# Hybrid S5 and mixture-of-experts step: the last batch's scatters ahead of slot 2's gather, slot 2's high products ahead of slot 1's low-weight products

## The chip, the core and the metric

The kernel runs on one core of a Trainium2 chip. The metric is the device time of one execution in microseconds. The engines named here are TensorE (PE in the rows), VectorE (DVE), ScalarE (ACT), GpSimd (POOL) and SyncE (SP), which here only issues transfers. Each engine works through its own instructions in the order in which the program writes them, and waits on semaphores for the others.

## The reference, cut to what matters

One decoder layer on 2112 tokens (2048 of a prompt, 64 of samples), width 1024, in float32: RMSNorm, a state-space mixer, a residual add, and then a mixture of experts in two levels with a final RMSNorm. The part that the change touches is the mixture:

```python
g_idx = jnp.argmax(pg, axis=-1)                # one of 4 groups
top_w, top_i = lax.top_k(pe, TOP_K)            # 2 of the 4 experts in it
eid = g_idx[:, None] * EXPERTS_PER_GROUP + top_i
h = silu(x @ w_gate[e]) * (x @ w_up[e])        # 1024 -> 256, for each of 16 experts
h = h * combine                                # weight of the token for that expert
out = h @ w_down[e]                            # 256 -> 1024
y = rmsnorm(x + out)
```

## The kernel before

The mixer comes first and ends in `x_mid` in HBM, the rows of all tokens, 17 tiles of at most 128 rows. In between, VectorE works out for each tile which two experts each token has and at which place in that expert's list the token stands.

**Records.** For each token and choice a record of five words (token, where the sum stands, where the output goes, weight, root) is written by an indirect transfer of GpSimd into a table `records` in HBM (`file_rows`, line 548). There are two such scatters for a tile, 34 in all, in four batches: tiles 0 to 5, 6 to 10, 11 to 14, and 15 and 16. A batch waits for the semaphore `idx_done`, which VectorE raises at line 2035 when the places (`at_rec`, line 2034) are known. SyncE reads columns of the table back into SBUF (`tab`, a part of `low`) in four loads, lines 453, 456, 458 and 459: the first two hold the records of slots 0, 1 and 2, since the places of the experts' first blocks fill up before all tiles are in; the last two hold the rest and wait until every scatter has landed.

**Slots.** The expert stage runs over slots of 128 rows, each of one expert. For slot `s`:

- `gather(s)` (line 575) on GpSimd takes the record column by `fetch` (line 564) and gathers 128 rows of `x_mid` into `xg`, ring of 8.
- `e_turn(s)` (line 1329) on TensorE transposes the rows in 8 matmuls against the identity (line 1338). For slot 1 it is `second_turn` (line 1349).
- `e_x(s)` (line 939) on ScalarE rounds the transposed rows to `xgH`, and `e_x_lo` on VectorE writes the remainder `xgL`. The weights are split likewise, into `WH` by `cut_hi` on ScalarE and `WL` by `cut_lo` on VectorE.
- The product up is a sum of three: `WH`*`xgH`, `WL`*`xgH` and `WH`*`xgL`, 8 matmuls each. In `e_up` these are `up_high` (the first two, lines 1404 and 1405) and `up_low` (line 1411). For slot 1 they are apart: `up_second_hi` (line 1359), and `up_second_lo` (lines 1365 and 1368).
- `e_silu`, `e_h` give `hh`; `e_hturn` (line 1418) transposes it in two matmuls (line 1423); `e_ht_hi` on ScalarE and `e_ht` on VectorE (line 1894) make `hTH` and `hTL`, and `e_down` (lines 1430 to 1432, 12 matmuls) gives the product down. VectorE adds it to the row (`e_sum`, line 2146), GpSimd scatters sums and outputs.

**The entry.** The first slots are written out by hand, since routing is still going on beside them. Their order is fixed by the program text alone; no scheduler moves anything. On TensorE, after the product down of slot 0, the text is: wait for the control words (`ctl_done`), transpose slot 2, the second half of slot 1's `WH`*`xgH`, then slot 1's `WH`*`xgL` and `WL`*`xgH`, slot 2's `up_high`, the transposes of slot 1's `hh`, slot 2's `up_low`, and slot 1's product down. On ScalarE, line 1002 (`cut_hi(0, 2)`, the third part of expert 1's weights) stands behind waits for all scatters, and `e_x(2, 0)` behind it. From slot 3 on `e_step` repeats.

Of the kernel before, what the change touches and what calls it, by code (L numbers as in the profile page):

```python
# [32 lines left out]
EPS = 1e-6  # L33
# [22 lines left out]
NEAR = 4 * TT  # L56
# [15 lines left out]
def hybrid_kernel(nc, x_rows, x_first, x_cols, s0, par, bc_in, d_in, gmix, gffn, gfin, w_in, w_out, w_route,  # L72
# [9 lines left out]
    with outer:  # L82
# [110 lines left out]
        for n in (0, 1):  # L193
# [68 lines left out]
        names = """par_in gm_in bc_in win0 win1 win2 win3 win4 win5 win6 win7 rt_in gl_in dch act_small c_g1 c_pool   # L262
# [5 lines left out]
            dchd exp_d consts tab_set tab_clear d_ready pos_done pos_read idx_done tab_early tab_in tab_first tab_ready tot_done words_set words_done ctl_done exp_in rec_set  # L268
# [38 lines left out]
        def _(sp):  # L307
# [150 lines left out]
            sp.dma_start(tab[:, 2:NEAR, :], table[:, 2:NEAR, :]).then_inc(S["tab_first"], 16)  # L458
# [9 lines left out]
        def _(pool):  # L468
# [5 lines left out]
            pool.memset(epsc[:, :], EPS).then_inc(S["c_pool"], 1)  # L474
            pool.memset(ones[:, :], 1.0).then_inc(S["c_pool"], 1)
# [88 lines left out]
            def fetch(t):  # L564

                if t == 3:
                    pool.wait_ge(S["tab_first"], 48)
                    pool.wait_ge(S["ctl_done"], 1)
                if t == AHEAD:
                    pool.wait_ge(S["tab_ready"], 16)  # L570
                col = pool.value_load(ctrl[0:1, C_COL + t:C_COL + t + 1], min_val=0, max_val=REC * (COLS - 1)) if t > 2 else (0, TT * REC, REC)[t]
                pool.tensor_copy(recs[:, t, :], tab[:, :, :].rearrange("p c w -> p (c w)")[:, ds(col, REC)]).then_inc(S["rec_set"], 1)
                pool.wait_ge(S["rec_set"], t + 1)
# [19 lines left out]
            for n, (lo, hi) in enumerate(BATCHES):  # L593
                if n == 2:

                    pool.wait_ge(S["tab_first"], 16)
                    pool.wait_ge(S["ys_lo"], 2 * TF)
                    for b in range(2):
                        pool.wait_ge(S[f"x2_st{b}"], 32 * ((FIRST_TOK + 1 - b) // 2) + 32 * (1 - b))
                    gather(0)  # L600

                    pool.wait_ge(S["a_done"], 4 * TF - 1)
                    gather(1)
                if n == 3:

                    pool.wait_ge(S["tab_first"], 32)
                    for b in range(2):
                        pool.wait_ge(S[f"x2_st{b}"], 32 * ((SECOND_TOK + 1 - b) // 2) + 32 * (1 - b))
                    gather(2)
                for t in range(lo, hi):  # L610
                    file_rows(t, n)

            pool.wait_ge(S["rl_evac"], TT)
# [94 lines left out]
        def _(act):  # L708
# [73 lines left out]
            act.wait_ge(S["c_pool"], 2)  # L782
# [217 lines left out]
            act.wait_ge(S["ctl_done"], 1)  # L1000
            act.wait_ge(S["wts2"], 32)
# [79 lines left out]
            e_x(2, 0)  # L1081
# [14 lines left out]
        def _(pe):  # L1096
# [77 lines left out]
            pe.wait_ge(S["c_pool"], 2)  # L1174
# [186 lines left out]
            def up_second_lo():  # L1361

                pe.wait_ge(S["xgt_lo"], 4)
                for k in range(KD):
                    pe.matmul(pbig[:, 6, :], xgL[1][:, k, :], WH[:, k * 2 * DE:(k + 1) * 2 * DE], start=False, stop=False)
                for k in range(KD):
                    pe.wait_ge(S["lo_split"], PIECES + k + 1)
                    mm = pe.matmul(pbig[:, 6, :], xgH[1][:, k, :], WL[:, EW + k * 2 * DE:EW + (k + 1) * 2 * DE], start=False, stop=(k == KD - 1))
# [212 lines left out]
        def _(dve):  # L1581
# [355 lines left out]
            dve.wait_ge(S["consts"], 10)  # L1937
# [283 lines left out]
            e_h(1, 1)  # L2221
            e_sum(0, 0)
            cut_lo(0, EW, 1, UP_CUTS)
            e_ht(1, 1)
# [77 lines left out]
```

## Time and profile before

| | us |
|---|---|
| median of 3 runs | 820.11 (818.72 to 821.96) |
| profiled execution | 819.82 |
| its span in the trace | 818.1 |
| TensorE busy in the span | 783.8 (96%) |
| VectorE busy | 597.6 (73%) |
| ScalarE busy | 409.8 (50%) |
| GpSimd busy | 341.4 (42%) |

The span is the time from the first to the last instruction in the trace; the profiled execution's time is 1.7 us longer than its span. The stage of the mixer ends and the stage of the slots begins between 405 and 450 us from the span's start; the last matmul is at 805 us. A row of the timeline gives the start, the time from start to end, the engine and line, and in square brackets the idle time of the engine before it with what ended it. Matmuls overlap, so the time between two starts is what one of them costs.

### The profile page before, as it was taken

To read this page: it belongs to the slowest core of one execution; us is meant where nothing else is said; L and a number is where in the kernel's file an instruction comes from. 1 tells how busy PE (TensorE), PEld (TensorE's weight loads), DVE (VectorE), ACT (ScalarE), POOL (GpSimd) and SP (SyncE) were. 2 spreads that over 40 slices of the span, in tenths; PEclk is the share of its full clock that TensorE was granted. 3 is DMA by queue.
4 is the path that set the end of the run, shared out by engine and by line. 5 is a ranking of instruction groups with operands and counts; after the bars stand their busy time and mean duration, and the time that the engine had idled before them with its cause. 6 is when DMAs were issued, how large, how long until landed. Compare 5 with 4: busy or idle time off the path is not lost.

```text
span 818.1 us, 15245 instructions
## 1 busy us (share of the span) xinstructions
PE 783.8 (96%) x4265; PEld 618.2 (76%) x4265; DVE 597.6 (73%) x1143; ACT 409.8 (50%) x770; POOL 341.4 (42%) x416
## 2 busy tenths in 40 slices
PE   6999989999999999999989999999999999999993
PEld 4888866655787787878767778888888888888882
DVE  7998789996543364556877598678786788776863
ACT  7556752124343543434353576546565566565632
POOL 3920011012000000322445567686766767676653
PEclk9999999999999999999999999999999999999997
DMA  8565315889742423424357588767866678877832
GB/s 306 159 228 185 129 28 186 215 160 209 287 155 81 152 107 126 133 101 155 105 208 250 184 302 259 249 208 248 273 224 227 231 260 285 291 238 233 280 121 106
DMA packets 57671, 161.27 MB, mean 197 GB/s; under 512 B 21856, under 2 KB 26464, under 8 KB 50912
## 3 DMA queue, kind: packets, MB, share of 16 engines
q1 hardware_dynamic: 34304, 112.99, 43.5%
q0 software_dynamic: 22976, 47.05, 16.5%
q8 instruction: 44, 0.72, 0.4%
q14 instruction: 59, 0.48, 0.2%
q10 hardware_dynamic: 288, 0.03, 0.0%
HBM read 129.07 MB, written 62.40 MB: 234 GB/s over the span
## 4 chain that ended last, share of the span: by engine, by line
PE 43%; POOL 2%; issue 2%; DVE 2%; DMA 1%; ACT 1%; DVEq 0%; POOLq 0%; ACTq 0%
PE pbig L1404 9%; PE pbig L1411 9%; PE pbig L1405 9%; PE pbig L1430 4%; PE pbig L1432 4%; PE pbig L1431 4%; PE pbig L1338 4%; POOL records L556 1%; PE pbig L1423 1%; DMA records<-rec,at_rec 1%; ACT xgH L944 0%; ACT pbig L1013 0%; DMA low<-records 0%; DVE fo L2137 0%; DVE xg L2146 0%
## 5 line engine op out<-in xcount | busy, mean ns | idle before, releaser
L1404 PE MATMUL pbig<-WH,xgH 128*128 (+1 forms) x304 | 123.0, 405 | 1.5 <-ACT xgH L944 0.9
L556 POOL DMA_INDIRECT records<-rec,at_rec x34 | 39.2, 1153 | 191.4 <-DVEq L2035 159.1
L1405 PE MATMUL pbig<-WL,xgH 128*128 (+1 forms) x304 | 118.9, 391 | 0.0
L1285 PE MATMUL pbig<-w2H,ysH 128*128 128x512 f32 x256 | 105.3, 411 | 0.0
L2042 DVE SCALAR_TENSOR_TENSOR WL<-WR,gf_p,WH 128x512 f32 (+1 forms) x128 | 87.4, 745 | 18.2 <-ACT WH L934 18.1
L1286 PE MATMUL pbig<-w2L,ysH 128*128 128x512 f32 x256 | 100.6, 393 | 0.0
L1287 PE MATMUL pbig<-w2H,ysL 128*128 128x512 f32 x256 | 100.5, 393 | 0.0
L630 POOL DMA_INDIRECT x_sums<-xg,recs x36 | 76.2, 2118 | 24.3 <-DVE xg L2146 13.1
L934 ACT ACTIVATE WH<-WR,gf_p 128x512 f32 (+1 forms) x128 | 81.8, 716 | 1.3
L952 ACT ACTIVATE sl<-pbig,recs 128x256 f32<-128x256 f32 x40 | 19.0, 475 | 117.8 <-PE pbig L1411 117.8
L1411 PE MATMUL pbig<-WH,xgL 128*128 (+1 forms) x304 | 77.1, 395 | 0.0
L1404 PEld LDWEIGHTS pbig<-WH,xgH 128*128 128x128 f32 x304 | 57.1, 188 | 15.3 <-issue 2.5
L1411 PEld LDWEIGHTS pbig<-WH,xgL 128*128 128x128 f32 x304 | 57.0, 188 | 13.6
L1430 PE MATMUL pbig<-WH,hTH 128*128 (+1 forms) x160 | 66.4, 415 | 0.5 <-DVE hTL L1894 0.5
L1405 PEld LDWEIGHTS pbig<-WL,xgH 128*128 128x128 f32 x304 | 57.0, 188 | 11.3
L1914 DVE TENSOR_TENSOR x<-pbig,sg 128x1024 f32<-128x1024 f32 x16 | 19.6, 1223 | 62.8 <-PE pbig L1287 61.4
L1432 PE MATMUL pbig<-WH,hTL 128*128 (+1 forms) x160 | 63.3, 396 | 0.0
L2137 DVE SCALAR_TENSOR_TENSOR fo<-xg,eroot,low 128x1024 f32<-128x1024 f32 x39 | 49.9, 1278 | 18.1 <-POOL eroot L653 18.1
L1431 PE MATMUL pbig<-WL,hTH 128*128 (+1 forms) x160 | 62.5, 390 | 0.0
L2146 DVE SCALAR_TENSOR_TENSOR xg<-pbig,recs,xg 128x1024 f32<-128x1024 f32 x39 | 49.9, 1278 | 15.1 <-PE pbig L1432 13.6
L1285 PEld LDWEIGHTS pbig<-w2H,ysH 128*128 128x128 f32 x256 | 48.2, 188 | 13.8 <-issue 4.6
L1880 DVE TENSOR_TENSOR xgL<-pbig,xgH 128x512 fp32r<-128x512 f32 x80 | 51.3, 681 | 8.0 <-ACT xgH L944 3.1
(356 smaller groups left out, 1710.6 us busy)
## 6 DMA issues: line engine op xcount, KB each, us to landing
WR<-in_w_gu SPq DMA_DIRECT2D x32, 1024.0 KB, 6.6
WR<-in_w_dn SPq DMA_DIRECT2D x16, 1024.0 KB, 5.9
xT<-in_x_cols SPq DMA_DIRECT2D x16, 512.0 KB, 3.8
low<-in_x_rows SPq DMA_DIRECT2D x16, 512.0 KB, 4.5
U<-in_x_rows SPq DMA_DIRECT2D x16, 512.0 KB, 5.3
x_mid<-x SPq DMA_DIRECT2D x16, 512.0 KB, 2.7
x_sums<-x SPq DMA_DIRECT2D x16, 512.0 KB, 4.5
w<-in_w_out SPq DMA_DIRECT2D x1, 4096.0 KB, 13.6
```

Of the source, the lines that this page charges most:

```text
L630: pool.indirect_dma_start(sumD, bass.IndirectOffsetOnAxis(ap=recs_u[:, t, SUM_AT:SUM_AT + 1], axis=0), xg[t % RING][:, :], None, bounds_ch ...
L934: act.activation(WH[:, ds(to + k * 2 * DE, 2 * DE)], WR[:, k * 2 * DE:(k + 1) * 2 * DE], ACT.Copy, scale=gf_p[:, k:k + 1]).then_inc(S["hi_ ...
L1285: pe.matmul(pbig[:, n, :], ysH[b][:, k, :], w2H[n][:, k, :], start=(k == 0), stop=False)
L1286: pe.matmul(pbig[:, n, :], ysH[b][:, k, :], w2L[n][:, k, :], start=False, stop=False)
L1287: mm = pe.matmul(pbig[:, n, :], ysL[b][:, k, :], w2H[n][:, k, :], start=False, stop=(k == CB - 1))
L1404: pe.matmul(out, xgH[b][:, k, :], WH[:, ds(off + k * 2 * DE, 2 * DE)], start=(k == 0), stop=False)
L1405: pe.matmul(out, xgH[b][:, k, :], WL[:, ds(low_ + k * 2 * DE, 2 * DE)], start=False, stop=False)
L1411: mm = pe.matmul(out, xgL[b][:, k, :], WH[:, ds(off + k * 2 * DE, 2 * DE)], start=False, stop=(k == KD - 1))
L1430: pe.matmul(out, hTH[b][:, k, :], WH[:, w], start=(k == 0), stop=False)
L1431: pe.matmul(out, hTH[b][:, k, :], WL[:, ds(low_ + at, 512)], start=False, stop=False)
L1432: mm = pe.matmul(out, hTL[b][:, k, :], WH[:, w], start=False, stop=(k == 1))
L2042: stt(WL[:, ds(low_ + w, 2 * DE)], WR[:, w:w + 2 * DE], gf_p[:, k:k + 1], WH[:, ds(to + w, 2 * DE)].bitcast(F32), ALU.mult, ALU.subtract). ...
```

## The change

Four places of the program text differ.

1. GpSimd: `gather(2)` (with its `fetch`) stood ahead of the fourth batch's four scatters; it now stands behind them. For that the third load of the table raises a semaphore of its own, `tab_near`, and two semaphores of the start (`c_pool`, `consts`) are made one.
2. ScalarE: `e_x(2, 0)` goes ahead of the last part of the weights' rounding, `cut_hi(0, 2)` and of its wait `wts2`. The waits for all scatters and for `ctl_done` still stand ahead of both.
3. TensorE: `up_second_lo` is cut in two: `up_second_x` (`WH`*`xgL`) and `up_second_w` (`WL`*`xgH`). Slot 2's `up_high` now comes between them, and the transposes of slot 1's `hh` come behind slot 2's `up_low` and straight ahead of slot 1's product down. The transposes of slot 2 (`e_turn(2, 2)`) stay where they were.
4. VectorE: `e_h(1, 1)` comes behind `e_sum(0, 0)` and the third part of `cut_lo`.

```diff
             sp.wait_ge(S["tab_in"], 16 * 2 * (TT - SECOND_TOK))
-            sp.dma_start(tab[:, 2:NEAR, :], table[:, 2:NEAR, :]).then_inc(S["tab_first"], 16)
+            sp.dma_start(tab[:, 2:NEAR, :], table[:, 2:NEAR, :]).then_inc(S["tab_near"], 16)
...
                 if t == 3:
-                    pool.wait_ge(S["tab_first"], 48)
+                    pool.wait_ge(S["tab_near"], 16)
...
-                if n == 3:
-
-                    pool.wait_ge(S["tab_first"], 32)
-                    for b in range(2):
-                        pool.wait_ge(S[f"x2_st{b}"], 32 * ((SECOND_TOK + 1 - b) // 2) + 32 * (1 - b))
-                    gather(2)
                 for t in range(lo, hi):
                     file_rows(t, n)
 
+            pool.wait_ge(S["tab_first"], 32)
+            for b in range(2):
+                pool.wait_ge(S[f"x2_st{b}"], 32 * ((SECOND_TOK + 1 - b) // 2) + 32 * (1 - b))
+            gather(2)
             pool.wait_ge(S["rl_evac"], TT)
...
             act.wait_ge(S["ctl_done"], 1)
+            e_x(2, 0)
             act.wait_ge(S["wts2"], 32)
             cut_hi(0, 2)
...
-            e_x(2, 0)
             e_silu(1, 1)
...
             up_second_hi(KD // 2, KD)
-            up_second_lo()
+            up_second_x()
             up_high(2, 0, EW, 0, 0)
+            up_second_w()
+            up_low(2, 0, EW)
             e_hturn(1, 1)
-            up_low(2, 0, EW)
             e_down(1, 1, 0, 1, EW)
...
             e_x_lo(2, 0)
-            e_h(1, 1)
             e_sum(0, 0)
             cut_lo(0, EW, 1, UP_CUTS)
+            e_h(1, 1)
             e_ht(1, 1)
```

GpSimd before, from the gather of slot 1 (`xg<-x_mid,low`) to the gather of slot 3; `records` is the table in HBM, `recs` the column taken from it:

```order
L588 DMA xg<-x_mid,low 128x1024
L572 COPY recs<-low 128x5
L556 DMA records<-rec,at_rec 34816x5 x8
L572 COPY recs<-low 128x5
L588 DMA xg<-x_mid,recs 128x1024
L556 DMA records<-rec,at_rec 34816x5 x4
L571 TENSOR_LOAD ctrl
```

GpSimd now, the same place:

```order
L588 DMA xg<-x_mid,low 128x1024
L572 COPY recs<-low 128x5
L556 DMA records<-rec,at_rec 34816x5 x12
L572 COPY recs<-low 128x5
L588 DMA xg<-x_mid,recs 128x1024
L571 TENSOR_LOAD ctrl
```

The four scatters of the fourth batch have joined the eight of the third, and the gather of slot 2 (`xg<-x_mid,recs`) has gone behind all twelve.

TensorE before, from the last matmul of slot 0's product down to the first pair of slot 2's `up_high`:

```order
L1432 MATMUL pbig<-WH,hTL0 128x512
L1338 MATMUL pbig<-ident,xg2 128x128 x8
L1359 MATMUL pbig<-WH,xgH1 128x512 x4
L1365 MATMUL pbig<-WH,xgL1 128x512 x8
L1368 MATMUL pbig<-WL,xgH1 128x512 x8
L1404 MATMUL pbig<-WH,xgH0 128x512
```

TensorE now, at the same place (line numbers of the changed program; the number behind a name is the buffer, and `xgH1` is slot 1's, `xgH0` slot 2's):

```order
L1433 MATMUL pbig<-WH,hTL0 128x512
L1336 MATMUL pbig<-ident,xg2 128x128 x8
L1357 MATMUL pbig<-WH,xgH1 128x512 x4
L1363 MATMUL pbig<-WH,xgL1 128x512 x8
L1405 MATMUL pbig<-WH,xgH0 128x512
```

The eight transposes of slot 2 are still the first thing behind slot 0's product down; what has left the place behind `WH`*`xgL` are the eight `WL`*`xgH` of slot 1.

TensorE before, from the last pair of slot 2's `up_high` to the start of slot 1's product down (`hTH`):

```order
L1404 MATMUL pbig<-WH,xgH 128x512
L1405 MATMUL pbig<-WL,xgH 128x512
L1423 MATMUL pbig<-ident,hh 128x128 x2
L1411 MATMUL pbig<-WH,xgL 128x512 x8
L1430 MATMUL pbig<-WH,hTH 128x512
```

TensorE now:

```order
L1405 MATMUL pbig<-WH,xgH 128x512
L1406 MATMUL pbig<-WL,xgH 128x512
L1369 MATMUL pbig<-WL,xgH 128x512 x8
L1412 MATMUL pbig<-WH,xgL 128x512 x8
L1424 MATMUL pbig<-ident,hh 128x128 x2
L1431 MATMUL pbig<-WH,hTH 128x512
```

Slot 1's eight `WL`*`xgH` stand behind `up_high` now, and between the transposes of `hh` and the product down that uses them no matmul is left.

## Rows read from the trace of the kernel before

**Rows 1.** The page: busy time by engine.
```profile
PE 783.8 (96%) x4265; PEld 618.2 (76%) x4265; DVE 597.6 (73%) x1143; ACT 409.8 (50%) x770; POOL 341.4 (42%) x416
```

**Rows 2.** Stretches: span, PE, PEld, DVE, ACT, POOL busy (instructions), granted clock, DMA, GB/s.
```profile
445.00:453.00 8.00, 7.34 (x36) 5.43 (x34) 2.75 (x5) 2.98 (x6) 4.71 (x7) 1.00 1.00 371
453.00:500.00 47.00, 45.34 (x215) 36.24 (x216) 38.94 (x52) 30.97 (x52) 30.78 (x32) 1.00 0.70 244
500.00:804.00 304.00, 303.99 (x1477) 249.14 (x1476) 232.92 (x297) 172.04 (x295) 208.51 (x217) 1.00 0.71 237
```

**Rows 3.** Timeline of TensorE, from slot 2's transposes to slot 1's product down.
```profile
433.08 1.03 PE L1338 MATMUL pbig<-ident,xg 128*128 128x128 f32 x8
...
434.89 2.02 PE L1365 MATMUL pbig<-WH,xgL 128*128 128x512 f32 x8
436.75 2.00 PE L1368 MATMUL pbig<-WL,xgH 128*128 128x512 f32 x8
439.20 0.51 PE L1404 MATMUL pbig<-WH,xgH 128*128 128x512 f32 x1 [0.45 <-ACT xgH L944]
...
443.02 0.38 PE L1423 MATMUL pbig<-ident,hh 128*128 128x128 f32 x2
443.15 2.11 PE L1411 MATMUL pbig<-WH,xgL 128*128 128x512 f32 x8
445.10 0.39 PE L1430 MATMUL pbig<-WH,hTH 128*128 128x512 f32 x1
```

**Rows 4.** Timeline of GpSimd: third batch's scatters, gather 2, fourth batch's.
```profile
410.46 1.02 POOL L556 DMA_INDIRECT records<-rec,at_rec  x1 [5.12 <-DVEq L2035]
...
420.39 0.96 POOL L556 DMA_INDIRECT records<-rec,at_rec  x1 [0.30 <-issue]
421.65 0.96 POOL L556 DMA_INDIRECT records<-rec,at_rec  x1 [0.31 <-issue]
427.94 0.19 POOL L572 COPY recs<-low 128x5 f32<-128x5 f32 x1 [5.33 <-DMA low<-records]
428.41 1.00 POOL L588 DMA_INDIRECT xg<-x_mid,recs  x1 [0.27 <-POOL recs L572]
429.71 0.98 POOL L556 DMA_INDIRECT records<-rec,at_rec  x1 [0.30 <-issue]
...
434.03 1.02 POOL L556 DMA_INDIRECT records<-rec,at_rec  x1 [0.30 <-issue]
```

**Rows 5.** Timeline of VectorE: the places of the third and the fourth batch.
```profile
409.44 0.17 DVE L2034 SCALAR_TENSOR_TENSOR at_rec<-high,place 128x8 uint32<-128x8 f32 x1
...
424.69 0.17 DVE L2034 SCALAR_TENSOR_TENSOR at_rec<-high,place 128x4 uint32<-128x4 f32 x1
```

**Rows 6.** Line 588: time from issue to landing of gather 2.
```profile
DMA to landing us min/median/max: 4.5/4.5/4.5
```

**Rows 7.** The same of gather 0, issued at 402.5, gather 1 behind it.
```profile
DMA to landing us min/median/max: 5.6/5.6/5.6
```

**Rows 8.** The same of gather 3, issued at 440.4.
```profile
DMA to landing us min/median/max: 7.8/7.8/7.8
```

**Rows 9.** Timeline of SyncE: the third load of the table, the weights of expert 2.
```profile
436.20 0.33 SPq L458 DMA_DIRECT2D low<-records  x1
...
437.10 0.85 SPq L443 DMA_DIRECT2D WR<-in_w_gu  x2
```

**Rows 10.** Timeline of ScalarE, behind the transposes of slot 1's hh.
```profile
443.43 0.38 ACT L958 ACTIVATE hTH<-pbig 128x256 fp32r<-128x256 f32 x1 [3.92 <-PE pbig L1423]
```

**Rows 11.** Timeline of VectorE, the same place.
```profile
443.85 0.42 DVE L1894 TENSOR_TENSOR hTL<-pbig,hTH 128x256 fp32r<-128x256 f32 x1
```

**Rows 12.** Timeline of TensorE: its longest wait between matmuls, and its last matmul.
```profile
12.97 0.50 PE L1115 MATMUL pbig<-w1H,xH 128*128 128x512 f32 x1 [1.73 <-ACT xH L722]
...
804.66 0.39 PE L1432 MATMUL pbig<-WH,hTL 128*128 x1
```

**Rows 13.** One stretch behind the last matmul, columns as in the second group.
```profile
808.00:809.00 1.00, 0.00 (x0) 0.00 (x0) 0.36 (x1) 0.00 (x0) 0.81 (x2) 0.53 0.00 0
```

More of the change, by code:

```diff
@@ L259, in hybrid_kernel @@
         wst.close()
-        names = """par_in gm_in bc_in win0 win1 win2 win3 win4 win5 win6 win7 rt_in gl_in dch act_small c_g1 c_pool
+        names = """par_in gm_in bc_in win0 win1 win2 win3 win4 win5 win6 win7 rt_in gl_in dch act_small c_g1
             x_in0 x_in1 xrow_in0 xrow_in1 w1_hi w1_lo xh_done xl_done sq_done std_done rin_done um_done us_done us8_in tr_done ue_act ue_dve
@@ L267, in hybrid_kernel @@
             wout_in w2_hi w2_lo ys_hi ys_lo a_done sig_done x2_done xr_in0 xr_in1 x2_st0 x2_st1 wr_scaled xt_done xt_evac lt_done lt_evac fold_set rl_done rl_evac ssq_done half_ss dchc
-            dchd exp_d consts tab_set tab_clear d_ready pos_done pos_read idx_done tab_early tab_in tab_first tab_ready tot_done words_set words_done ctl_done exp_in rec_set
+            dchd exp_d consts tab_set tab_clear d_ready pos_done pos_read idx_done tab_early tab_in tab_first tab_near tab_ready tot_done words_set words_done ctl_done exp_in rec_set
             gat0 gat1 gat2 gat3 xgt_done xgt_evac xgt_lo gu_done h_done sl_done ht_done ht_evac hi_split lo_split dn_done dn_evac wts0 wts1 wts2
@@ L473, in _ @@
             ch(pool.memset(power[:, :], -0.5))
-            pool.memset(epsc[:, :], EPS).then_inc(S["c_pool"], 1)
-            pool.memset(ones[:, :], 1.0).then_inc(S["c_pool"], 1)
+            pool.memset(epsc[:, :], EPS).then_inc(S["consts"], 1)
+            pool.memset(ones[:, :], 1.0).then_inc(S["consts"], 1)
             ch(pool.memset(upper[:, :], 1.0))
@@ L781, in _ @@
             act.activation(AN[:, 4, :, :], AN[:, 2, :, :], ACT.Sin).then_inc(S["act_small"], 1)
-            act.wait_ge(S["c_pool"], 2)
+            act.wait_ge(S["consts"], 2)
             for t in range(1, TA):
@@ L1172, in e_spread @@
                 mm.then_inc(S["et_done"], 1)
-            pe.wait_ge(S["c_pool"], 2)
+            pe.wait_ge(S["consts"], 2)
             a_first()
@@ L1359, in up_second_hi, with up_second_x @@
                     pe.matmul(pbig[:, 6, :], xgH[1][:, k, :], WH[:, k * 2 * DE:(k + 1) * 2 * DE], start=(k == 0), stop=False)
-            def up_second_lo():
+            def up_second_x():
                 pe.wait_ge(S["xgt_lo"], 4)
@@ L1365, in up_second_lo, with up_second_w @@
                     pe.matmul(pbig[:, 6, :], xgL[1][:, k, :], WH[:, k * 2 * DE:(k + 1) * 2 * DE], start=False, stop=False)
+            def up_second_w():
                 for k in range(KD):
@@ L1936, in _ @@
             dch = Chain(dve, S["dchd"])
-            dve.wait_ge(S["consts"], 10)
+            dve.wait_ge(S["consts"], 2 + 10)
             dch(dve.memset(logit[LAST:P, 0, :], 0.0))
```

## The prediction

> **What bounds the kernel now.** I read the page's busy times first: TensorE is busy for 96% of the span, no other engine above 73% [rows 1]. Such a share is a mean, so the stretches come next. From 500 to 804 us TensorE is busy for 303.99 of 304 us at the full clock; from 445 to 500 it lacks only 0.66 + 1.66 = 2.3 us [rows 2]. Whatever delays TensorE before 445 us therefore arrives at the end nearly whole, and whatever lets it go earlier is gained nearly whole. The change touches 425 to 450 us, so its worth is read from the order of things on TensorE there. That timeline is dense: slot 2's transposes start at 433.08 straight behind slot 0's product down, and the one wait up to slot 1's product down at 445.10 is 0.45 us before slot 2's first product, for `xgH` from ScalarE [rows 3]. By starts: the eight matmuls of `WL`*`xgH` take 1.86 us (as the eight of `WH`*`xgL` do, 434.89 to 436.75), and 436.75 + 1.86 = 438.61, so the wait costs 0.59 us. The chain of waits goes back from this wait over the fourth batch's scatters and GpSimd's gather of slot 2 to routing, and so makes GpSimd look like the bound of this place. It is so only for 0.59 us. What else hangs on GpSimd is the gather itself: issued at 428.41 [rows 4], landed 4.5 us later [rows 6], at 432.9. TensorE asks for it at 433.08. So gather 2 has a spare of 0.2 us and no more.
>
> **GpSimd: scatters ahead of the gather.** The four scatters wait for `at_rec`. In the third batch VectorE ended it at 409.44 + 0.17 = 409.61 and the first scatter began at 410.46, 0.85 us later. The fourth batch's ends at 424.69 + 0.17 = 424.86 [rows 5], so the first scatter would begin at 425.7, in an idle time of GpSimd of 5.33 us [rows 4]. From start to start undisturbed scatters take 1.26 us (420.39 to 421.65), so the fourth begins at 425.7 + 3.8 = 429.5 and ends at 430.5. If they stretch as they did before, 434.03 - 429.71 = 4.3 us instead of 3.8, it is 431.0. Then comes the copy of the record, 0.47 us from its start to the gather's (427.94 to 428.41): the gather is issued at 431.0 (to 431.5), 2.6 us later than before. The load of the column it needs had come at 427.9 and is no limit.
>
> How long does it take to land? Alone it took 4.5 us [rows 6]. Now it has company. The last scatter would land by 429.5 + 2.2 = 431.7 (before: issued 434.03, and SyncE's load of the table that waits for it began at 436.20 [rows 4, 9]), and the two loads of the table move at the same time as the gather's rows, where before they went out after it had landed. Bounds: 4.5 us alone; 7.8 us for gather 3, which had the table and two megabytes of weights beside it [rows 8, 9]. The nearest case is gather 0, with another gather of its size behind it: 5.6 us [rows 7]. I take 5.5. It lands at 436.5 and the transposes start at 436.6, 3.5 us later than 433.08. With 4.5 us it would be 2.4 to 2.9 us late, with 7.8 it would be 5.8.
>
> TensorE executes in order, and `e_turn(2, 2)` is still its first work behind slot 0's product down. Behind it stand slot 1's second half of `WH`*`xgH`, its `WH`*`xgL` and `WL`*`xgH`, all of which could run, and none can pass it. So the 3.5 us are a wait and nothing fills it.
>
> The Trainium skill, page "DMA: Bandwidth & Descriptors", section "Queues, rings and completion order", says that each transfer engine takes turns between the queues that have work for it. By that rule the gather shares with the two table loads and is slower than alone; by the row of gather 2 alone it would not be. The rows of gathers 0 and 3 side with the page.
>
> **TensorE and ScalarE: slot 2's high products first.** With the wait for all scatters gone 4 us earlier, ScalarE begins `e_x(2, 0)` as soon as the transposes are there, and about 2.9 us of matmuls (half of `WH`*`xgH` and `WH`*`xgL`) cover it. So the 0.59 us go away. From the start of the transposes to that of slot 1's product down it took 445.10 - 433.08 = 12.02 us. Without the wait and without the two transposes of `hh` (443.02 to 443.15, 0.13) that leaves 11.3 us of matmuls. Then come the transposes of `hh`, now with nothing behind them to cover what follows: `hTH` began 0.41 us after their start and took 0.38 [rows 10], `hTL` began at 443.85 and ended at 444.27 [rows 11], plus 0.06 us for TensorE to go on, in all 1.3 us from their start to the product down. Sum 11.3 + 1.3 = 12.6, or 12.5 without the slower first matmul behind the old wait: 0.5 us more than before. The change takes away one wait of 0.59 and makes one of about 1.2 (1.3 less the transposes' own 0.13). Bounds: 0 if all of it is covered after all, 1.0 if VectorE is late with `hTL`.
>
> **The rest at nothing.** ScalarE's `cut_hi(0, 2)` ends some 2 us later than before, about 440; `WL`'s third part follows on VectorE by 443, and slot 1's product down needs it at 449. VectorE's `e_h(1, 1)` moves behind the sum and that part: slot 1's product up ends only at about 445.7 now, so nothing waits for the order. `hh` is ready by 446.8, while `up_low` of slot 2 runs to 447.6. If that cover were gone (VectorE 1 us later) it would cost nothing still. The table's last loads and so gathers 3 and 4 go 4 us earlier; gather 3, issued at 440.4, landed at 448.2, just when it was wanted, and has spare now. The merged semaphore costs nothing: the same two increments are awaited.
>
> **The sum.** 3.5 + 0.5 = 4.0 us. The profiled execution is 819.82 us, its span 818.1, and the 1.7 us between them stay. So 823.8; the median of the runs is 820.11, 0.3 above it, and I predict 824.1. A measurement of this kernel can tell about 0.5%, 4.1 us, from no change: the forecast stands at that line.
>
> **Rivals.**
> *The clock falls in the wait.* The longest wait of TensorE between its matmuls was 1.73 us [rows 12], and the clock stayed full. Behind its last matmul, begun at 804.66, the granted clock has a mean of 0.53 in 808 to 809 [rows 13]: it fell to 1.2 GHz 3 us after the work had ended. A wait of 3.5 us reaches that. The work behind it then runs at half speed until the clock is back. If that lasts as long as the fall took, 3 us, it costs 1.5; if it lasts over everything up to `up_high` (436.75 - 433.08 = 3.7 us of work), 3.7. I take 2: 826.1. For it speaks the tail; against it that the wait lies between two dense stretches, which the tail does not. By the Trainium skill, page "TensorE: Matmul & The Clock Gate", section "Why this matters for your kernels", gaps in TensorE's work between bursts of matmuls can bring it back to half rate, and a wait of this size would be such a gap; the tail agrees, and the wait of 1.73 us was too short to show it.
>
> *The gather lands as late as gather 3.* 7.8 us: 5.8 + 0.5 = 6.3, 826.4. For it: scatters and two loads in flight. Against it: the weights of expert 2 wait for VectorE and would join only at its end.
>
> *Absorbed.* The gather is hardly late (the scatters' descriptors are made faster beside an idle VectorE, it lands in 4.5 us), and some of the 2.3 us of waits from 445 to 500 go: 2.5 + 0.5 - 1.5 = 1.5, 821.6. Against it: those waits are for `hh` and `xgH`, which follow TensorE itself.
>
> *Faster: the gather in time.* If the scatters' data is out of the way and the gather's rows come before TensorE has done with slot 0, the wait at the transposes is nought, the 0.59 goes, the gap before the product down is covered, and with gathers 3 and 4 and the weights 2 to 4 us earlier all 2.3 us of later waits go too: 2.9 less, 817.2. It decides at a landing by 433.1, 2.1 us after an issue at 431.0; the shortest gather here took over 4.
>
> **How the numbers follow.** Forecast 55% (its own range 822.7 to 825.2), clock 25%, late gather 8%, absorbed 7%, faster 5%. Slower by over 0.5% (above 824.2): 0.4 of the forecast's 55, nine tenths of the clock's 25, the late gather: 0.22 + 0.22 + 0.08 = 0.52. Faster: 0.05. Within 0.5%: 0.43. Range for 8 in 10: 822.0, between absorbed and the forecast's low end, to 827.0, above the clock and the late gather.
>
> **What would show it.** TensorE's row of slot 2's transposes has a wait of 2.4 to 4.5 us, for the gather; gather 2 is issued near 431.0, behind four scatters from 425.7; `up_high` of slot 2 has no wait for `xgH`; the first matmul of slot 1's product down has one of about 1 us, for `hTL`; from 500 us on everything is the same, shifted. A granted clock below 1.00 near 437 shows the first rival. No wait at the transposes, or a gather issued before 430, would prove the forecast wrong; so would waits of 2 us gone between 445 and 500.

## The result and the profile after

The changed kernel takes 823.22 us (median of 20 runs, 820.96 to 829.35), the kernel before 820.65 (20 runs beside them). The ratio is 1.0036, with a 95% interval from 1.0023 to 1.0049: slower by 0.36%, or 3.0 us. That is the forecast's direction, 0.9 us below the predicted 824.1, inside its range, and on this side of the 0.5% line.

The profiled execution took 824.25 us with a span of 822.5, 4.4 us more than the span before, and the busy times are nearly those of [rows 1]:

```profile
PE 785.8 (96%) x4265; PEld 619.2 (75%) x4265; DVE 597.9 (73%) x1143; ACT 409.8 (50%) x770; POOL 338.6 (41%) x416
```

The two spans can't be subtracted as they stand. Slot 0's product down, the last work on TensorE ahead of the change's place, begins at 430.18 us in the trace before and here at 432.36: 2.18 us of the 4.4 had arisen before the place where the orders differ. Over the thirteen traces of this study that start lies anywhere from 429.21 to 435.15 us, so what the merged semaphore of the start does to it, if anything, can't be told. So I measure every kernel of this study from that start. The *entry stretch* runs from the start of slot 0's product down to the start of slot 1's.

TensorE after, start, time, line, and the idle time with its cause, where [rows 3] stood before:

```profile
432.36 0.50 PE L1431 MATMUL pbig<-WH,hTH 128*128 128x512 f32 x1
...
437.37 1.07 PE L1336 MATMUL pbig<-ident,xg 128*128 128x128 f32 x8 [1.97 <-issue]
438.19 1.18 PE L1357 MATMUL pbig<-WH,xgH 128*128 128x512 f32 x4
439.21 2.02 PE L1363 MATMUL pbig<-WH,xgL 128*128 128x512 f32 x8
441.07 0.40 PE L1405 MATMUL pbig<-WH,xgH 128*128 128x512 f32 x1
...
444.76 2.01 PE L1369 MATMUL pbig<-WL,xgH 128*128 128x512 f32 x8
446.61 2.04 PE L1412 MATMUL pbig<-WH,xgL 128*128 128x512 f32 x8
448.49 0.38 PE L1424 MATMUL pbig<-ident,hh 128*128 128x128 f32 x2
449.80 0.50 PE L1431 MATMUL pbig<-WH,hTH 128*128 128x512 f32 x1 [0.93 <-DVE hTL L1896]
```

Three things are to be seen. TensorE waits 1.97 us at slot 2's transposes. The matmul at 441.07, slot 2's first product, waits for nothing. The product down at 449.80 waits 0.93 us for `hTL`. The entry stretch is 449.80 - 432.36 = 17.44 us; before it was 445.10 - 430.18 = 14.92. The place costs 2.52 us.

The wait at the transposes is written "issue", the name for a wait whose releaser the profile doesn't show. GpSimd tells what it is ([rows 4] before):

```profile
427.29 0.96 POOL L556 DMA_INDIRECT records<-rec,at_rec  x1 [2.58 <-DVEq L2037]
...
431.08 0.95 POOL L556 DMA_INDIRECT records<-rec,at_rec  x1 [0.31 <-issue]
432.03 0.20 POOL L572 COPY recs<-low 128x5 f32<-128x5 f32 x1
432.51 1.00 POOL L588 DMA_INDIRECT xg<-x_mid,recs  x1 [0.27 <-POOL recs L572]
```

The four scatters stand between 427.29 and 432.03, 1.26 us from start to start, and gather 2 behind them. Its time from issue to landing ([rows 6]):

```profile
DMA to landing us min/median/max: 4.8/4.8/4.8
```

432.51 + 4.8 = 437.3, and the transposes start at 437.37. The chain that ended last has the wait as a link of its own, which before it had not at this place:

```profile
435.40 1.97 issue
437.37 1.07 PE pbig L1336 x8
```

The granted clock of the wait and of the work behind it, and of the dense part ([rows 2]):

```profile
433.00:439.00 6.00, 4.03 (x23) 3.15 (x22) 5.87 (x10) 0.88 (x2) 0.64 (x2) 1.00 0.79 233
504.00:808.00 304.00, 303.88 (x1474) 248.84 (x1473) 232.78 (x297) 171.88 (x294) 207.46 (x216) 1.00 0.71 237
```

The clock stayed at 2.4 GHz through the wait, and behind 504 us all is as it was, shifted.

### The profile page after: what moved, and what is told of

It reads as the page before. It is cut to its first block, busy times and chain, and to the rows that moved or that the text cites. A ratio compares the mean times of both kernels' runs of the same rounds, so it can differ in the third digit from the quotient of the medians.

```text
span 822.5 us, 15244 instructions
## 1 busy us (share of the span) xinstructions
PE 785.8 (96%) x4265; PEld 619.2 (75%) x4265; DVE 597.9 (73%) x1143; ACT 409.8 (50%) x770; POOL 338.6 (41%) x416
## 4 chain that ended last, share of the span: by engine, by line
PE 43%; DVE 4%; issue 2%; ACT 1%; POOL 0%; DVEq 0%; ACTq 0%; POOLq 0%
PE pbig L1405 9%; PE pbig L1412 8%; PE pbig L1406 8%; PE pbig L1431 4%; PE pbig L1433 4%; PE pbig L1432 4%; PE pbig L1336 4%; PE pbig L1424 1%; DVE fo L2139 0%; ACT pbig L1012 0%; ACT WH L932 0%; PE pbig L1363 0%; PE pbig L1369 0%; ACT WH L935 0%; DVE xg L2148 0%
## 5 line engine op out<-in xcount | busy, mean ns | idle before, releaser
L628 POOL DMA_INDIRECT x_sums<-xg,recs x36 | 74.1, 2058 | 23.2 <-DVE xg L2148 13.8
L621 POOL DMA_INDIRECT xg<-x_sums,recs x36 | 49.9, 1385 | 17.6 <-issue 12.9
```

The lines of the kernel that those rows point to most:

```text
L628: pool.indirect_dma_start(sumD, bass.IndirectOffsetOnAxis(ap=recs_u[:, t, SUM_AT:SUM_AT + 1], axis=0), xg[t % RING][:, :], None, bounds_ch ...
```

## The experiments

All numbers of the kernels side by side, from one profiled execution each; the last column is the ratio to the kernel before with its interval where the kernel was timed. Starts are those of products down: "entry" from slot 0's to slot 1's, "2 to 3" from slot 2's to slot 3's, "to last" from slot 0's to the last matmul of all.

| kernel | wait at slot 2's transposes | entry | 2 to 3 | to last | ratio |
|---|---|---|---|---|---|
| before | none | 14.92 | 17.83 | 374.48 | |
| e9_before_again | none | 14.92 | 17.44 | 373.73 | |
| after | 1.97 | 17.44 | 17.02 | 376.63 | 1.0036 [1.0023, 1.0049] |
| e1_gpsimd_alone | 1.68 | 16.05 | 17.01 | 374.82 | 1.0020 [0.9998, 1.0042] |
| e2_other_engines_alone | none | 16.06 | 17.00 | 375.94 | 1.0015 [0.9995, 1.0034] |
| e3_tensore_undone | 2.02 | 16.41 | 17.10 | 374.89 | |
| e4_turn_behind | none | 14.19 | 17.03 | 373.19 | 0.9991 [0.9975, 1.0007] |
| e5_two_ahead | none | 14.36 | 16.99 | 373.42 | 0.9987 [0.9970, 1.0004] |
| e7_table_later | 1.68 | 17.18 | 17.03 | 375.74 | |
| e6_act_first | none | 14.29 | 17.54 | 373.22 | |
| e11_act_first_timed | none | 14.23 | 17.70 | 373.45 | 0.9994 [0.9982, 1.0007] |
| e8_two_ahead_act_first | none | 14.19 | 17.01 | 372.53 | 0.9983 [0.9969, 0.9998] |
| e10_gather_later | 4.70 | 22.48 | 17.04 | 382.53 | |

The entry stretch of the kernel before came out at 14.92 twice, so its tenths mean something. "To last" differs by 0.75 us between two traces of one and the same kernel, so there only differences above that do.

### One half of the change at a time

My theory, A in the expectations: gather 2 is late by the scatters, and the order on TensorE adds a gap. The rival, B: the order on TensorE is what costs. The first experiment keeps GpSimd's change alone (TensorE's part of the edit is shown; `e_x(2, 0)` on ScalarE and `e_h(1, 1)` on VectorE are back in their old places too):

```diff
 after, with TensorE, ScalarE and VectorE in the order of before:
-            up_second_x()
-            up_high(2, 0, EW, 0, 0)
-            up_second_w()
-            up_low(2, 0, EW)
-            e_hturn(1, 1)
+            up_second_x()
+            up_second_w()
+            up_high(2, 0, EW, 0, 0)
+            e_hturn(1, 1)
+            up_low(2, 0, EW)
```

> The kernel before with the GpSimd part of the change alone (gather 2 behind the fourth batch's scatters); ScalarE, VectorE and TensorE in the order of before. The entry stretch, from the start of slot 0's product down to that of slot 1's, is 14.92 us before and 17.44 in the changed kernel. Theory A (the late gather makes TensorE wait about 2.1 us at slot 2's transposes, the wait of 0.59 us for xgH goes, the new order of the products costs about 0.9 on its own): stretch 14.92 + 2.1 - 0.6 = 16.4 us, time 1.5 us above before, a wait of about 2 us at the transposes, none ahead of slot 1's product down. Rival B (the new order of the products is what costs, the gather's delay alone is harmless): stretch 14.9, no wait at the transposes.

Measured: 821.92 us. TensorE's row of the transposes, and the gather:

```profile
436.81 1.06 PE L1336 MATMUL pbig<-ident,xg 128*128 128x128 f32 x8 [1.68 <-issue]
```
```profile
432.22 0.99 POOL L588 DMA_INDIRECT xg<-x_mid,recs  x1 [0.27 <-POOL recs L572]
```

The wait is there with TensorE's old order, so it comes from GpSimd. The entry stretch is 16.05: 1.13 us more than before. That is the wait and what else the lateness moves (436.81 - 432.07 = 4.74 from slot 0's product down to the transposes, 2.90 before: 1.84), less 0.71 us behind it, for the wait for `xgH` (0.59) and the slow first matmul behind it are gone. The rest to the changed kernel is 17.44 - 16.05 = 1.39 us: 0.27 of it the later transposes (5.01 against 4.74), 1.12 the changed order on the other engines.

The second experiment keeps that order and puts the gather back ahead of the scatters:

```diff
 after, on GpSimd:
+                if n == 3:
+                    pool.wait_ge(S["tab_first"], 32)
+                    ...
+                    gather(2)
                 for t in range(lo, hi):
                     file_rows(t, n)
```

> The changed kernel with gather 2 put back ahead of the scatters; the new orders of TensorE, ScalarE and VectorE stay. Theory A: transposes without a wait; xgH of slot 2 still waits for the last scatter on ScalarE (some 6 us behind the start of slot 0's product down), so a wait of about 0.6 us ahead of slot 2's first product; a gap of about 0.9 us ahead of slot 1's product down, for hTL. Stretch about 16.0 us, time 1.1 us above before. Rival B: stretch near 17.4, time as the changed kernel.

Measured: 821.17 us, an entry stretch of 16.06. TensorE shows no wait at the transposes of slot 2, but three others:

```profile
437.01 0.50 PE L1407 MATMUL pbig<-WH,xgH 128*128 128x512 f32 x1 [0.40 <-ACT xgH L944]
...
445.83 0.50 PE L1433 MATMUL pbig<-WH,hTH 128*128 128x512 f32 x1 [0.93 <-DVE hTL L1898]
...
450.25 1.09 PE L1338 MATMUL pbig<-ident,xg 128*128 128x128 f32 x8 [1.14 <-DMA xg<-x_mid,recs]
```

The first is the old one: `e_x(2, 0)` still stands behind the waits for all scatters, and these are late again. The second is the new gap of the order, to the hundredth that of the changed kernel. The third I had not foreseen; it is gather 3 and has its own section below. So each half costs 1.13 to 1.14 us in the entry stretch. Their sum, 2.27, is near the whole, 2.52; neither theory alone holds the full cost, and B as the only cause is out. This rests on the traces: the timed runs of the two (ratios 1.0020 and 1.0015) have intervals that just reach 1.

The third experiment takes just TensorE's order out of the changed kernel (`up_second_w` ahead of `up_high`, the transposes of `hh` ahead of `up_low`), and leaves ScalarE and VectorE changed:

```diff
 after, on TensorE:
+            up_second_w()
             up_high(2, 0, EW, 0, 0)
-            up_second_w()
-            up_low(2, 0, EW)
             e_hturn(1, 1)
+            up_low(2, 0, EW)
```

> The changed kernel with TensorE's order of before (slot 1's WL*xgH ahead of slot 2's high products, the transposes of hh ahead of slot 2's low products); GpSimd, ScalarE, VectorE as changed. Theory A (the new order of products costs the gap of 0.93 us ahead of slot 1's product down and gives nothing beyond what ScalarE's earlier xgH gives): a wait of 1.7 to 2 us at the transposes stays, no wait for xgH, no gap: entry stretch 16.1 to 16.5 us against 17.44 in the changed kernel. Rival (the new order pays for itself by covering xgH): stretch 17.4 or more, with a wait ahead of slot 2's high products.

```profile
435.44 1.06 PE L1336 MATMUL pbig<-ident,xg 128*128 128x128 f32 x8 [2.02 <-issue]
```

The wait is the changed kernel's, no gap stands ahead of the product down, and the stretch is 16.41: 1.03 us less than with TensorE's new order. The wait for `xgH` is gone here too, so the new order was not needed against it.

### Is it the transposes' place in the order?

If it is the wait for the gather, it must go once TensorE has other work ahead of the transposes. The work is there: slot 1's second half of `WH`*`xgH` and its `WH`*`xgL`.

```diff
 after, on TensorE (and e_h(1, 1) ahead of e_sum(0, 0) on VectorE):
-            e_turn(2, 2)
             up_second_hi(KD // 2, KD)
             up_second_x()
+            e_turn(2, 2)
+            up_second_w()
             up_high(2, 0, EW, 0, 0)
-            up_second_w()
-            up_low(2, 0, EW)
             e_hturn(1, 1)
+            up_low(2, 0, EW)
```

> The changed kernel with slot 2's transposes behind slot 1's second half of WH*xgH and its WH*xgL, then slot 1's WL*xgH, slot 2's high products, the transposes of hh, slot 2's low products; VectorE's hh of slot 1 where it stood before. GpSimd and ScalarE as changed. Theory A (the wait is one of order: 2.9 us of matmuls that could run stand behind the transposes): no wait at the transposes, none for xgH, no gap ahead of slot 1's product down; stretch 14.2 us, 0.7 under before and 3.2 under the changed kernel; time 0.7 us under before. Rival C (what the late gather costs shows again later, since gathers 3 and 4 and the sums are late too): stretch 14.2 but the time not below before.

```profile
436.97 1.03 PE L1336 MATMUL pbig<-ident,xg 128*128 128x128 f32 x8
437.76 2.10 PE L1369 MATMUL pbig<-WL,xgH 128*128 128x512 f32 x8
```

No idle time stands behind the row of the transposes. The entry stretch is 14.19, shorter than before by 0.73, with GpSimd exactly as in the changed kernel. Timed it is 819.68 us, ratio 0.9991 [0.9975, 1.0007], not told from the kernel before: the scatters ahead of the gather cost nothing that can be seen when TensorE's order has work for the time.

### Two scatters ahead, two behind

The other way to mend it, on GpSimd alone. `gather(2)` waits for its table column, which had come at 427.94 [rows 4]; two scatters fit into that idle time.

```diff
 before, on GpSimd:
-                if n == 3:
-                    ... gather(2)
                 for t in range(lo, hi):
+                    if t == lo + 1 and n == 3:
+                        ... gather(2)
                     file_rows(t, n)
```

> The kernel before with two of the fourth batch's four scatters ahead of gather 2 and two behind it; all other engines as before. Theory A: the two fit into GpSimd's idle time before the column of the table arrives, so the gather is issued as early as before and nothing waits at the transposes; the last scatter is issued 2.5 us earlier, so the wait of 0.59 us for xgH goes: stretch 14.3, time 0.6 us under before. Rival D (any scatter ahead of the gather delays it, through the transfers' queue): a wait of about 1 us at the transposes, stretch 15.3.

```profile
431.42 0.95 POOL L556 DMA_INDIRECT records<-rec,at_rec  x1 [0.30 <-issue]
433.07 0.19 POOL L572 COPY recs<-low 128x5 f32<-128x5 f32 x1 [0.70 <-DMA low<-records]
433.54 0.99 POOL L588 DMA_INDIRECT xg<-x_mid,recs  x1 [0.27 <-POOL recs L572]
```

Both scatters were over 0.70 us before the column came, so they don't hold the gather up. It landed in 4.6 us, with no wait at the transposes and an entry stretch of 14.36. The time is 819.27 us, ratio 0.9987 [0.9970, 1.0004], not told from the kernel before. What the change's idea is worth, scatters earlier, is here without its price.

### Do the table loads slow the gather?

In the changed kernel the gather lands in 4.8 us with two table loads beside it. Here these two wait until it has landed:

```diff
 after, on SyncE, ahead of the last two loads of the table:
+            sp.wait_ge(S["gat2"], 16)
             sp.wait_ge(S["tab_in"], 16 * 2 * (TT - SECOND_TOK))
```

> The changed kernel with the last two loads of the table held back until gather 2 has landed. Gather 2 took 4.8 us from issue to landing in the changed kernel, 4.5 alone in the kernel before. Theory A (beside the two loads the gather is 0.3 us slower): landing 4.5 us, the wait at the transposes 0.3 us shorter, stretch 17.1. Rival (its time is its own, and 4.5 to 4.8 is scatter): landing 4.8, stretch 17.4.

The gather landed in 4.5 us and the wait was 1.68:

```profile
435.19 1.06 PE L1337 MATMUL pbig<-ident,xg 128*128 128x128 f32 x8 [1.68 <-issue]
```

So loads that follow the gather cost it 0.3 us at most, and perhaps nothing: in e1, with the same loads beside it, it also landed in 4.5 us, so the rival of scatter isn't excluded. It is the loads that paid. The last two large ones before, 425 to 439 us (count, size, median us from issue to landing):

```profile
low<-records SPq DMA_DIRECT2D x1, 510.0 KB, 4.0
low<-records SPq DMA_DIRECT2D x1, 165.0 KB, 2.3
```

And after, in the same stretch:

```profile
low<-records SPq DMA_DIRECT2D x1, 510.0 KB, 5.2
low<-records SPq DMA_DIRECT2D x1, 165.0 KB, 4.3
```

With the loads held back (e7) they took 3.6 and 2.7 us. In the changed kernel they are issued 0.9 and 1.3 us behind the gather. In e10, further down, they go 0.8 and 0.45 us ahead of it, and there it is the gather that is slow, 5.6 us, while they take 3.7 and 2.8. Two other things are at work in that 5.6: the gather's issue took 1.47 us instead of 1.00, and the weights of expert 2 joined from 436.58, before it had landed. In one trace, then, who pays turned with who was issued first; no run separates the three.

### The old wait by itself, and gather 3

The wait for `xgH` (0.59 us) that the change takes away stands there because ScalarE does `e_x(2, 0)` behind the waits for all scatters. One line moved takes it away too:

```diff
 before, on ScalarE:
+            e_x(2, 0)
             act.wait_ge(S["tab_early"], 16 * 2 * SECOND_TOK)
             act.wait_ge(S["tab_in"], 16 * 2 * (TT - SECOND_TOK))
             act.wait_ge(S["ctl_done"], 1)
...
-            e_x(2, 0)
             e_silu(1, 1)
```

> The kernel before with one edit: ScalarE takes slot 2's xgH ahead of its waits for the scatters. Gather 2 ahead of the scatters, TensorE and VectorE as before. Theory A (the 0.59 us wait of before was ScalarE's order alone, and needed nothing of GpSimd): no wait at the transposes, none for xgH, stretch 14.3 us. Rival: xgH still late, stretch 14.9.

One execution took 817.58 us. So I timed it, with the kernel before once more as a measure of what one trace can tell:

> The kernel with ScalarE's xgH of slot 2 ahead of its waits for the scatters, all else as before, now timed against it. Its one look had stretch 14.29 us and, from slot 0's product down to the last matmul, 373.2 us against 374.5 and 373.7 of before. Theory A: 0.6 us under before, ratio 0.9993, hardly to be told from 1. Rival: the single look's 3 us are real, ratio 0.9965.

> The kernel before once more, nothing changed, for its trace. From slot 2's product down to slot 3's it took 17.83 us, with a wait of 0.55 us ahead of slot 3's first product; the changed kernel and four variants take 17.0. Theory E (a lasting trait of the kernel before, so the changed kernel gains 0.8 us there): 17.8 again. Rival F (it differs from execution to execution): 17.0.

The entry stretch is 14.29 and 14.23, 0.6 to 0.7 below before, as expected; but the times say 819.86 us, ratio 0.9994 [0.9982, 1.0007], and the 817.58 was luck. The stretch from slot 2's product down to slot 3's took 17.44 us in the second trace of before: neither 17.8 nor 17.0, so the wait in it is a trait of the kernel whose size varies. In both kernels with ScalarE's edit a wait has come up at slot 3's transposes (e11):

```profile
449.36 1.09 PE L1338 MATMUL pbig<-ident,xg 128*128 128x128 f32 x8 [0.48 <-DMA xg<-x_mid,recs]
```

Gather 3 can't be issued before the table's last loads, and these wait for all scatters. In the kernel before it lands at 448.2, just when it is wanted; a TensorE that is earlier by 0.6 us waits for it (0.75 us in e6, 0.48 in e11). In e2, with late scatters too, it was 1.14. There something else was added: the column's copy ahead of gather 3 took 2.17 us on GpSimd, beside a VectorE instruction of 2.29. GpSimd's row and VectorE's:

```profile
439.61 2.17 POOL L572 COPY recs<-low 128x5 f32 x1 [4.95 <-issue]
```
```profile
439.44 2.29 DVE L2051 TENSOR_TENSOR WL<-WR,WH 128x2048 fp32r<-128x2048 f32 x1
```

How much of such a wait reaches the next product? From slot 1's product down to slot 2's it takes 4.65 and 4.64 us in the two traces of before, where slot 2's product down has to wait for `hTL` (0.46 and 0.61 us) even with the transposes in time. It takes 4.65 in e11 too, 4.75 in e6 and 5.27 in e2. So the waits of 0.48 and 0.75 us cost 0 and 0.1, and that of 1.14 some 0.6. The spare that earlier scatters give gather 3 is worth no more than that. What e6 and e11 share with the kernel before is another wait, ahead of slot 3's first product (0.29 and 0.42 us); it is explained further down, under "The rest at nothing".

### Both together

Two scatters ahead of the gather, two behind, and ScalarE's line moved: the edits of e5 and e6 on the kernel before.

> The kernel before with two of the fourth batch's scatters ahead of gather 2, two behind it, and ScalarE's xgH of slot 2 ahead of its waits for the scatters. Theory A: each edit alone removes the same 0.59 us wait, so together they give no more than one: stretch 14.3 us as with either alone. The last scatters land 2 to 3 us earlier, so the table and gathers 3 and 4 come earlier, and the wait of 0.3 to 0.5 us ahead of slot 3's first product, seen in the kernel before twice and with ScalarE's edit alone, goes as in the run with two ahead: from slot 2's product down to slot 3's 17.0 us. Time 1.0 us under before. Rival: the edits add up, stretch 13.7.

819.53 us, ratio 0.9983 with an interval from 0.9969 to 0.9998: faster than the kernel before, by little, and the one variant whose interval stays below 1. Against the changed kernel that makes 0.5% (0.9983/1.0036, an estimate from two ratios taken apart). The entry stretch is 14.19, no more than e4 reached, since both edits work at the same 0.59 us. From slot 2 to slot 3 it takes 17.01.

### Can the clock fall?

The rival on the clock did not show at a wait of 1.97 us. In this kernel (e10) the gather also waits until all scatters have landed, which makes the wait longer:

```diff
 after, on GpSimd, ahead of gather(2):
+            pool.wait_ge(S["tab_early"], 16 * 2 * SECOND_TOK)
+            pool.wait_ge(S["tab_in"], 16 * 2 * (TT - SECOND_TOK))
             gather(2)
```

> The changed kernel with gather 2 also waiting until all scatters have landed, 1.4 us later again. Theory A (TensorE's wait follows the gather one for one, the clock stays): wait 3.4 us at the transposes, stretch 18.8, granted clock 1.00 from 430 to 460. Clock rival (a wait that long brings the clock down as the end of the kernel does 3 us after the last matmul): granted clock under 1.00 in or behind the wait, matmuls of 128x512 at more than the 0.23 us from start to start, stretch 19.8 or more.

The wait became 4.70 us, and the entry stretch 22.48, not what theory A gave. The gather was issued 2.11 us behind the start of slot 0's product down (0.15 in the changed kernel) and landed in 5.6 us. TensorE:

```profile
439.56 1.94 PE L1338 MATMUL pbig<-ident,xg 128*128 128x128 f32 x8 [4.70 <-issue]
441.15 2.06 PE L1359 MATMUL pbig<-WH,xgH 128*128 128x512 f32 x4
443.01 2.70 PE L1365 MATMUL pbig<-WH,xgL 128*128 128x512 f32 x8
445.55 0.39 PE L1407 MATMUL pbig<-WH,xgH 128*128 128x512 f32 x1
```

And stretches of it, the granted clock in the third column from the end:

```profile
434.00:436.00 2.00, 0.86 (x4) 0.38 (x2) 2.00 (x4) 0.00 (x0) 1.39 (x1) 1.00 0.84 240
437.00:437.50 0.50, 0.00 (x0) 0.00 (x0) 0.50 (x2) 0.00 (x0) 0.18 (x1) 1.00 0.68 229
437.50:438.00 0.50, 0.00 (x0) 0.00 (x0) 0.50 (x2) 0.00 (x0) 0.25 (x1) 0.66 1.02 418
438.00:440.00 2.00, 0.44 (x2) 0.47 (x3) 1.15 (x2) 0.00 (x0) 1.73 (x3) 0.50 0.86 326
...
444.00:445.00 1.00, 1.00 (x5) 0.82 (x4) 1.00 (x2) 0.00 (x0) 0.13 (x1) 0.76 1.00 418
```

TensorE had been idle from 434.86. By these rows the clock left the full level between 437.5 and 438 (a mean of 0.66 puts it near 437.7), 2.8 us after TensorE had gone idle. It was at 1.2 GHz (0.50) from 438 and came back in 444 to 445. From the transposes to slot 2's first product it took 445.55 - 439.56 = 5.99 us instead of 441.07 - 437.37 = 3.70 in the changed kernel: the slow clock cost 2.3 us on top of the longer wait, 4.70 - 1.97 = 2.73. 2.73 + 2.29 = 5.02, and the stretch grew by 5.04. So the rival's mechanism is real here, and the price taken for it (2 us) was about right; it did not show in the changed kernel because the wait came out at 1.97 us and not at 3.5. No kernel with a wait of 3.5 us was run, but in this trace the fall came 2.8 us into the wait. A wait of 3.5 would have reached it.

## Why the prediction was right or wrong

**The path, right.** "Whatever delays TensorE before 445 us arrives at the end nearly whole": the entry stretch grew by 2.52 us, "to last" by 2.15 against the first trace of before and 2.90 against the second, and the measured times by 3.0. The traces don't place what the 3.0 has above them. E4 and e5, with the entry shorter by 0.7 and 0.6, have medians below before, though neither interval excludes 1; e8, shorter by 0.7 and with the short stretch behind it, is told from before.

**The late gather, right in kind, 1.4 us too long.** The forecast had the transposes 3.5 us late; measured from slot 0's product down they are 437.37 - 432.36 - 2.90 = 2.11 late. That is below even the forecast's lower bound of 2.4, and the wait of 1.97 us lies outside the 2.4 to 4.5 that was to show the forecast. Two terms were mis-sized:

- *"The first scatter began 0.85 us later" than the end of `at_rec`.* I took the third batch's lag for the fourth. It was 427.29 - 426.96 = 0.33 us there. VectorE's next instruction tells the two apart. In the kernel before, behind the third batch's `at_rec`:

```profile
410.31 1.23 DVE L1914 TENSOR_TENSOR x<-pbig,sg 128x1024 f32<-128x1024 f32 x1 [0.70 <-DVE at_rec L2034]
```

  and behind the fourth's:

```profile
425.01 0.48 DVE L1887 SCALAR_TENSOR_TENSOR hh<-pbig,recs,sl 128x256 f32<-128x256 f32 x1 [0.16 <-DVE at_rec L2034]
```

  In the changed kernel these two are at 412.42 (0.70 again) and 427.11 (0.16). The first scatter began 0.15 us behind VectorE's next start in before (410.46 - 410.31), and 0.16 and 0.18 behind it in the changed kernel (412.58 - 412.42, 427.29 - 427.11). By these three the 0.85 was 0.70 on VectorE's side and 0.15 for the handover, and the row from which 0.3 for the fourth batch could be read stood in the trace of before. It is a pattern of three batches; why VectorE pauses 0.70 us there isn't in the trace.
- *"I take 5.5" for the landing.* It was 4.8 (4.8 in e3 and e4 too, 4.5 in e1), against 4.4 to 4.6 in the kernels where nothing joins it: the table loads add 0.3 us at most where they follow the gather. My row for it, gather 0 with a gather behind it [rows 7], was the wrong neighbour; the bound by [rows 6] was the right value. Both gathers go through GpSimd's one queue, so that row couldn't show turns between queues either.

0.52 + 0.7 = 1.2 of the 1.4. Of the rest, 0.08 is that `at_rec` came earlier against slot 0's product down than before (5.40 us ahead of it instead of 5.32), and 0.1 is the forecast's rounding upwards. The pieces that were read straight from rows held: four scatters at 1.26 us, 0.48 from the copy to the gather.

The Trainium skill, page "DMA: Bandwidth & Descriptors", section "Queues, rings and completion order", says that each transfer engine takes turns between the queues that have work. The trace agrees that they share, but not in who pays as I had drawn from it: the gather lost 0 to 0.3 us, the table loads issued behind it 1.2 and 2.0.

**TensorE's own order, right.** The wait for `xgH` went and a gap for `hTL` came. From the transposes of `hh` to the product down it took 449.80 - 448.49 = 1.31 us (forecast 1.3), from slot 2's transposes to it 12.43 (forecast 12.6). The order costs 0.41 in the changed kernel. E3 says what this term leaves out: 1.03 us are lost against TensorE's old order, for with the scatters early the old order has neither wait nor gap. The change traded one wait for a larger gap where moving one line on ScalarE (e6), or two of the four scatters (e5), takes the wait away and makes none.

**"The rest at nothing", wrong to the good.** The stretch from slot 2's to slot 3's product down took 17.83 and 17.44 us in the two traces of before, 17.54 and 17.70 in e6 and e11, and 16.99 to 17.10 wherever the scatters are earlier. So the changed kernel gets back 0.4 to 0.8 us there. In before it is a wait ahead of slot 3's first product:

```profile
453.35 0.50 PE L1404 MATMUL pbig<-WH,xgH 128*128 x1 [0.55 <-issue]
```

The kernel's text says what stands there: ahead of slot 3's products TensorE loads three control words into registers, `words(3)`. In the kernel before:

```profile
L1532 PEldq TENSOR_LOAD <-ctrl x1: 1020/1020/1020, 449.8 to 449.8; - x1
L1533 PEldq TENSOR_LOAD <-ctrl x1: 708/708/708, 451.2 to 451.2; - x1
L1534 PEldq TENSOR_LOAD <-ctrl x1: 301/301/301, 452.3 to 452.3; - x1
```

And the first of them in e8:

```profile
L1535 PEldq TENSOR_LOAD <-ctrl x1: 482/482/482, 449.4 to 449.4; - x1
```

The product starts 1.05 us behind the start of the third load here, and 1.10, 1.06 and 1.02 in e9, e6 and e11, the other traces with a long stretch. In the nine with a short one it starts 1.25 us or more behind it, straight behind the product down: there the words come in time. The first load took 1.02, 0.84, 1.24 and 1.28 us in the four, and 0.48 to 0.49 in all nine. So the wait is for the control words, and what the changed kernel gets back is that they load faster. Why they do is open. E2 has late scatters and fast loads, so it isn't the scatters as such, and the load on the transfer engines tells little: in the 8.2 us from slot 1's product down its share is 1.01 in before and 0.96 in e8. One thing goes along with it: in the four traces GpSimd had issued its latest gather 1.4 to 2.0 us ahead of the first load, in the nine 2.9 us or more. That it is the cause was not tried.

**The chances.** 0.52 on slower by over 0.5% was too much. The forecast's middle stood on the line, and both terms with wide bounds, lag and landing, had been taken at or near a worse case than the nearest row of the same thing. With 0.33 and 4.5 the same sum gives 3.5 - 0.5 - 1.0 + 0.5 = 2.5 us.

**The rivals.** The clock rival fell for this change and holds for a longer wait (e10). The late gather and the gather in time fell on the landing of 4.8 us. "Absorbed" was right in part: the landing was near its 4.5 us, and 0.4 to 0.8 us of later waits went where it had 1.5. Its reason for an earlier gather, faster scatters, did not come: they kept their 1.26 us.

**Where luck helped.** By e10 the clock falls 2.8 us into a wait, so the forecast's own wait of 3.5 us at the full clock would not have stayed at the full clock: had the gather been as late as forecast, the time would have gone on towards the first rival's 826.1. That the clock stayed full is due to the gather being earlier than forecast. The direction and the cause were right by the rows; that 824.1 is only 0.9 us from the measured time is in part luck.

## What to carry to other kernels

Before moving work ahead of a transfer, look at which engine asks for the transfer and what stands behind that request in its order: here the same four scatters cost 2.1 us of lateness with the transposes first, and nothing with two groups of matmuls put ahead of them or with only as many scatters ahead as fit into the idle time (e4, e5). When bounding a lag or a landing, take the same instruction in its own place as the nearest row, and look whether the lag of a neighbour belongs to the sender. A wait on the dense engine has a price beyond its length once it is long enough for the clock to fall: none at 1.97 us here, 2.3 us on top at 4.70, where the clock fell 2.8 us into the wait. And a wait that the profile calls "issue" can be a register load: list the loads of the control words by their tile before leaving it open.

## What the hardware showed that was not expected

GpSimd's small instructions stretch to the length of a VectorE instruction beside them. In the changed kernel, GpSimd and VectorE:

```profile
440.58 0.20 POOL L572 COPY recs<-low 128x5 f32 x1
...
442.02 2.33 POOL L572 COPY recs<-low 128x5 f32 x1
```
```profile
442.03 2.28 DVE L2049 TENSOR_TENSOR WL<-WR,WH 128x2048 fp32r<-128x2048 f32 x1
```

The same copy of 128 by 5 words took 0.20 us beside a VectorE operation with one input in PSUM (`xgL`, 439.64 to 440.92) and 2.33 beside one that reads both its inputs from SBUF. In the kernel before it met the issue of gather 4 beside the same operation (VectorE 441.49 to 443.77):

```profile
442.05 2.57 POOL L588 DMA_INDIRECT xg<-x_mid,recs  x1 [0.48 <-POOL recs L572]
```

2.57 us instead of 1.00, ending 0.85 us behind the VectorE operation. The Trainium skill, page "SBUF — State Buffer", section "Who interferes with whom", says that a VectorE instruction with two inputs in SBUF contends with a GpSimd instruction that reads SBUF, and calls the port pair that they share an exclusive lock. The trace agrees: the copy ended with the VectorE operation. In e2 this fell on gather 3 and was part of a wait of 1.14 us on TensorE, of which some 0.6 us reached slot 2's product down: this is how such a collision can reach the dense engine.
